# One gate chunk placed behind the keys' latent transposes, and the last output chunk behind the last query transposes

## The reference

```python
h = rmsnorm(x, p["g_attn"])
proj = h @ p["w_in"]          # S5 input | query latent 384 | kv latent 256 | rope key 32 | memory query | 3 gates of 1024
br_a, h_re, h_im = s5_branch(u, h0_re, h0_im, p)
c_kv = rmsnorm(kv_lat, p["g_kvlat"])
q = mla_queries(q_lat, pos, p)                # rmsnorm(q_lat) @ w_uq, norm by head, rotary part
k, v = mla_keys_values(c_kv, k_pe, pos, p)    # c_kv @ w_ukv, norm by head, rotary part
br_b = o.reshape(b_, l_, MLA_WIDTH) @ p["w_o_mla"]
br_c = memory_attention(q_mem, mem_k, mem_v, p)            # ends in  o @ p["w_o_mem"]
gates = jax.nn.sigmoid(g_logit).reshape(b_, l_, N_BRANCHES, D_MODEL)
merged = gates[..., 0, :] * br_a + gates[..., 1, :] * br_b + gates[..., 2, :] * br_c
x = x + merged @ p["w_out"]
x = x + hierarchical_moe(rmsnorm(x, p["g_ffn"]), p)        # 4 groups of 8 experts, top 1 and top 2
```

## Time and profile before

| | |
|---|---|
| median of 3 runs | 638.8 us (636.69 to 639.08) |
| profiled execution | 638.72 us |
| its span, first to last instruction | 636.9 us |
| PE busy | 606.7 us, 95% of the span |
| DVE, ACT, POOL busy | 50%, 29%, 23% |
| mean granted PE clock | 0.992 of full speed |
| DMA | 150.57 MB, mean 236 GB/s |

### The profile page before, as it was taken

One profiled execution on the slowest core, in us unless ns is written; L12 is line 12 of the kernel. 1 busy time (PEld: TensorE's weight loads), 2 busy tenths in 40 slices (PEclk: granted clock), 3 DMA queues, 4 the chain that ended last, 5 costly groups with the idle time before them and its releaser, 6 DMA issues.

```text
span 636.9 us, 10034 instructions
## 1 busy us (share of the span) xinstructions
PE 606.7 (95%) x3742; PEld 378.3 (59%) x3742; DVE 321.1 (50%) x858; ACT 184.0 (29%) x579; POOL 149.1 (23%) x341
## 2 busy tenths in 40 slices
PE   8999999999999999999999999999999999887994
PEld 7888867777456667666677767854434443333441
DVE  3343947757883589772043222685524425425133
ACT  5534224532478445432100101212121121210100
POOL 1596627733584524510000000000000000000000
PEclk9999999999899999999999999999999999999899
DMA  9783553212301343323589990199999999999993
GB/s 302 180 289 108 193 171 100 68 66 84 113 2 33 127 139 100 100 67 100 150 255 395 404 388 20 38 369 415 417 416 415 418 415 417 418 416 418 412 408 112
DMA packets 61683, 150.57 MB, mean 236 GB/s; under 512 B 12352, under 2 KB 40448, under 8 KB 53696
## 3 DMA queue, kind: packets, MB, share of 16 engines
q1 hardware_dynamic: 61632, 149.89, 63.5%
HBM read 147.12 MB, written 2.76 MB: 235 GB/s over the span
## 4 chain that ended last, share of the span: by engine, by line
PE 89%; DVE 4%; issue 2%; DMA 2%; ACT 1%; SPq 0%; DVEq 0%
PE PS L832 28%; PE PS L842 21%; PE PS L1216 9%; PE PS L1113 7%; PE PS L1255 5%; PE PS L1245 5%; PE PS L958 2%; PE PS L915 2%; DVE X L2117 2%; PE PS L983 2%; PE PS L825 1%; PE PS L1166 1%; PE PS L1025 1%; DMA W<-in_w_in 1%; PE PS L966 1%
## 5 line engine op out<-in xcount | busy, mean ns | idle before, releaser
L832 PE MATMUL PS<-hT,W 128*128 128x320 f32 x416 | 117.2, 436 | 0.0
L832 PEld LDWEIGHTS PS<-hT,W 128*128 128x128 f32 x416 | 77.5, 190 | 33.4 <-issue 3.8
L1216 PE MATMUL PS<-E,xT 128*32 128x256 f32 (+1 forms) x1088 | 60.1, 374 | 8.5 <-issue 8.1
L1216 PEld LDWEIGHTS PS<-E,xT 128*32 128x32 f32 x1088 | 37.5, 112 | 35.5 <-issue 20.2
L2191 POOL TENSOR_SCALAR means<-sums 128x4 f32<-128x4 f32 (+3 forms) x35 | 7.6, 217 | 188.0 <-ACT junk L1358 187.1
L1113 PE MATMUL PS<-h,S 128*128 128x512 f32 (+1 forms) x96 | 48.2, 625 | 0.7 <-DVE S L1974 0.7
L1255 PE MATMUL PS<-yb,WG 128*128 128x512 f32 (+1 forms) x96 | 40.9, 622 | 4.0 <-DVE X L2117 3.1
L842 PE MATMUL PS<-W,hT 128*128 128x256 f32 (+5 forms) x256 | 41.7, 353 | 0.0
L2117 DVE TENSOR_TENSOR X<-X,PS 128x512 f32<-128x512 f32 (+1 forms) x48 | 32.8, 686 | 8.3 <-PE PS L1255 6.7
L842 PEld LDWEIGHTS PS<-W,hT 128*128 128x128 f32 (+1 forms) x256 | 31.5, 163 | 8.4 <-issue 1.3
L842 PE MATMUL PS<-W,mergedT 128*128 128x384 f32 (+3 forms) x192 | 35.7, 381 | 0.0
(11 more groups left out here) (313 smaller groups left out, 976.9 us busy)
## 6 DMA issues: line engine op xcount, KB each, us to landing
E<-in_w_e SPq DMA_DIRECT2D x93, 1024.0 KB, 21.3
W<-in_w_in SPq DMA_DIRECT2D x7, 1536.0 KB, 7.2
W<-in_w_in SPq DMA_DIRECT2D x7, 1024.0 KB, 8.6
W<-in_w_mem_kv SPq DMA_DIRECT2D x4, 1024.0 KB, 6.2
W<-in_w_glu SPq DMA_DIRECT2D x4, 768.0 KB, 7.7
W<-in_w_out SPq DMA_DIRECT2D x2, 1536.0 KB, 15.6
X<-in_x_prompt SPq DMA_DIRECT2D x4, 512.0 KB, 4.6
W<-in_w_o_mem SPq DMA_DIRECT2D x1, 1536.0 KB, 6.6
```

Source lines behind the costliest of these rows:

```text
L832: ins = mm(out[:, 0:TOK], w[:, k, cols:cols + 128], rhs[:, k, :], start=(k == 0), stop=(k == kt - 1))
L1216: ins = mm(PS[r:r + B, 2 + par, 128 * which.start:128 * which.stop], xT[:, k, place_ + B * n:place_ + B * n + B], E13[slot][:, which, k, 1 ...
```

## The change

In `middle()`, the line that puts all remaining `gateC` chunks ahead of the latent transposes now leaves one of them, and that one is put behind the `ckT` steps. And the list of steps at which an `outC` chunk is put between the head transposes loses its last entry, so that the last `outC` chunk is put after the loop.

```diff
     for t in range(NT):
         put("norm_ql", t)
         put("norm_ck", t)
-    fill(KD)
-    fills = [("outC", d) for d in range(KD)]
+    while len(fills) > 1:
+        fill()
     for t in range(NT):
         put("qlT", t)
     for j in range(len(KEYS)):
         put("ckT", j)
+    fill(KD)
+    fills = [("outC", d) for d in range(KD)]
     for n in range(len(KQ_UNITS) + KQ_LAG):
         held = n >= 5
         if n < len(KQ_UNITS):
             put("kq", n)
-        if n in (4, 7, 10, 13, 15, 17, 18, 19):
+        if n in (4, 7, 10, 13, 15, 17, 18):
             fill()
         if 0 <= n - NORM_LAG < len(KQ_UNITS):
             put("norm_kq", n - NORM_LAG)
         if n >= KQ_LAG:
             put("kqT", n - KQ_LAG)
     fill(KD)
```

## The result

The changed kernel takes 643.30 us (median of 4 runs, 643.04 to 644.09), the kernel before beside it 638.01 (636.69 to 639.08): a ratio of 1.0089, 95% interval 1.0068 to 1.0110, which is 5.3 us by the medians and 5.7 by the ratio. The profiled execution took 643.43, its span is 641.5 us against 636.9.

The account below looks back on a forecast made before the run. PE, busy 95% of the span, was taken to bound the kernel. First edit 5.08 - 0.73 + 0.3 + 0.5 = + 5.15, second - 0.56: + 4.6 on 638.72 gives 643.3 us, range 641.0 to 645.3.

Parts of the forecast that it names:

- What bounds: PE bounds; before `ckT` 2 it waits for ACT's `qlT` copy behind ten stores, and goes on at 164.72 as before.
- under cover of the stores: Before 164.72, `gateC` 7 and turn 8, 5.08 us of work, are done while the stores finish; 0.77 us is left unused.
- Moved work, + 5.08: `gateC` 7 (4.34 us) and turn 8 (0.74) leave the cover of the stores and lengthen PE's path before `kq` 0.
- the covered wait, - 0.73: PE's 0.73 us wait for ACT's copy of the last `ckT` is covered by `gateC` 7.
- The clock, + 0.3: Clock falls before PE goes on: `ckT` 2 to 4 end 0.3 us later, then some 3.25 us of work at half.
- DVE behind turn 8, + 0.5: Later turn 8 delays DVE's key scaling `norm_kq` 4, needed by `kqT` 4: 0 to 0.9 us, taken as 0.5.
- The second edit, - 0.56: Before the first scores, `outC` 7 behind `kqT` 15 hides PE's 0.56 us wait for ACT's copy to `qT`.
- The load of `gateB0`: Lands at 222.6, wanted at 223.1 after the first scores and turn 10; 0.5 us are left, so it costs nothing.
- What reaches the end: + 4.6 us reaches the end: the experts' weight stream is tied to PE and nothing absorbs a delay.
- the empty DMA stretch: From 384 to 408 us DMA engines moved nothing, all expert buffers full; taken as showing that no delay is absorbed later.
- Rival 2: Around the `ckT` steps, clock stays up or falls later: + 2.7 to + 3.2 us in sum, 641.4 to 641.9; chance 0.13.
- rival 3: Clock stays down longer, or DVE's delay grows behind turn 9: + 1.1 to + 2.2 us more, 644.4 to 645.5; chance 0.15.

Follow-up runs that it names:

- e3: Changed kernel, with the four memory key and value stores on their own semaphore, so ACT's first `qlT` copy waits only for those: 640.03 us, 1.0039 of before.
- e4: Kernel before, with the four memory key and value stores on their own semaphore, so ACT's first `qlT` copy waits only for those: 635.90 us, 0.9976 of before.
- e7: Changed kernel plus 11 matmuls of no use in PE's three gaps, to keep the clock up: 640.08 us, 1.0040 of before.
- e5: Kernel before with only turn 8 moved behind the `ckT` steps, one of them ahead of its PE work; `gateC` 7 stays: 638.71 us, 1.0015 of before.
- e1: Changed kernel with the `outC` edit undone, so only `gateC` 7 and turn 8 are moved: 643.48 us, 1.0099 of before.
- e9: Kernel before plus 3 matmuls of no use, 2 ahead of `ckT` 2 and 1 ahead of `kq` 0: 636.73 us, 0.9988 of before.

## Why the prediction was right

- **What bounds.** PE's restart at 164.72 came to 164.69, with the releaser named. e3 shows by removing it that the wide wait for the stores was what held it. But the prediction has `gateC` 7 and turn 8 "under cover of the stores", and that is half of it: without the wide wait PE still stands 3.10 us for DVE's norms, and the change still costs 4.1 us (e3 against e4). The sum came out all the same, since of the two waits the stores' ends last.
- **Moved work, + 5.08, and the covered wait, - 0.73.** Restart to `kq` 0 went from 1.78 to 8.49 us. Of the 6.71 more, 5.08 - 0.73 are this term; e7, with a full clock, has 6.23 - 1.78 = 4.45 against 4.35.
- **The clock, + 0.3.** Mis-sized. The direction was right, the clock fell before PE went on. But it was at half for 6.83 us and not for 3.41, so the transposes lost 0.4 (1.42 us from their start to that of the next row, and 0.99 at full clock in e5) and `gateC` 7 lost 2.0 (6.33 instead of 4.34), 2.4 together against the 1.6 that `kq` 0 to 4 had lost: + 0.8. The estimate took the length of the stretch of work at half clock from one fall, 3.25 us; here 5.15 us of work, from 164.69 to 169.84, ran at half.
- **DVE behind turn 8, + 0.5.** Wrong by this much: it was 0. `norm_kq` 4 began 21.7 behind `kq` 0 and not 23.3. Of the 23.1 us counted as work, 0.28 was a wait for POOL ahead of the scaling at 173.49. And the work of DVE between these points isn't a constant: the first part of turn 8, up to the end of its scans, took 4.6 us before and 4.2 in the changed kernel, and the six instructions of turn 9's way back 4.0 and 3.3. In the slower cases more of POOL's table work ran beside them; that it is the cause was not tested.
- **The second edit, - 0.56.** It was - 0.85: from `kqT` 14 to the scores there were 3.69 us, and are 2.84. The rows tell where the other 0.3 lie: the wait from start to start is 0.62 and not 0.56, `kqT` 14 and 15 side by side take 0.58 where they took 0.72 apart, and `outC` 7 takes 2.26 instead of 2.35. The load of `gateB0` didn't take it back.
- **What reaches the end.** PE's 5.08 at the next turn less 0.85 is 4.2 at the first scores, and 4.24 at 415.23: nothing was absorbed, as the empty DMA stretch said.

The errors of + 0.5, - 0.5 and - 0.3 in the terms cancelled in part: 4.2 where 4.6 had been said, and another 0.4 in the expert stage, which no experiment took apart. That the two profiled executions are 4.7 us apart (643.43 and 638.72), and the median exactly 643.3, is therefore partly luck; the largest term, the work moved less the covered wait, is not: 4.45 in e7 against 4.35. Against the median the change is 5.3 and not 4.6, because the median of before had moved from 638.8 to 638.01 with a fourth run. Rival 2 (the clock stays up) didn't occur in the profile of the changed kernel; rival 3's clock part occurred, smaller than its + 1.1, and without its DVE part.

## What to carry to other kernels

Independent work is worth most where PE would wait for something outside PE, and the idle time left in such a place says how much more could be put there, not how much can be taken away: before moving a chunk out, find what ends the wait behind it, and whether that moves too. There can be two such waits, one behind the other: removing the later one uncovers the earlier. So the price of a change has to be compared between two kernels that both lack the wait. A semaphore that counts more than what the memory needs makes a wait out of an unrelated result; counting the stores apart was worth 1.5 us to the kernel before, for an edit that moves no work. And runs of one and the same kernel differ here by 2 to 3 us, more than the smaller effects looked for, so a price read off one profile has to be held against timed runs; a mean clock says that the clock fell, and not where.

## What the runs showed of the hardware

The time at half clock around the gap was 0, 3.41, 6.83 or 10.24 us in the eleven profiles. It didn't follow the length of the gap alone: e1 and the changed kernel have the same order of work there, and the clock fell at 161.6 in the one and at 163.0 in the other; e5, with a still stretch of 1.67 us, kept it in its profile, and before, with 0.77 and 0.73, lost it. With a few matmuls of no use in the gaps it stayed up in the profiles of both kernels that had them; the mean clock of e7's five runs was 0.995 to 0.997, against 0.984 to 0.992 in the changed kernel, that of e9's twelve 0.992 to 0.997. For e9 that alone proves little, since e5's profile kept the clock without them. The Trainium skill ("TensorE: Matmul & The Clock Gate", Part 1: The HAM clock gate) says that where the transition falls varies from run to run of one kernel; the traces of e1 and the changed kernel agree, with falls at 161.6 and 163.0 us at the same place of the same order; in the runs of before the time varied from 636.58 to 639.41 us and the mean clock from 0.990 to 0.996.
